# Differential-attention layer: the turn of the fourth attention tile placed behind the low parts of v, the turn of the gated rows one slot sooner, and the weighted values in two PSUM banks

## The chip, the cores and the metric

The kernel runs on one NeuronCore of a Trainium2 chip. The metric is the device time of one execution in microseconds (us). The execution that the profiler recorded has its own time; the rows below are from it.

## What is computed

The reference is one decoder layer over 512 rows of 2048 float32 values. It is cut here to what matters:

```
proj = x @ w_in                           # [512, 4*2048]: q | k | v | z
# 8 head pairs; in each two heads of q and k (128 wide) and one v, z (256 wide)
logits = q_h @ k_h.T / sqrt(128) + rel_bias[distance], causal
a = softmax(logits_0) - lam * softmax(logits_1)
o = a @ v                                 # [512, 256] for each pair
o = rms_norm(o, subln_g) * (1 - lam_init)
y = (o * silu(z)) @ w_out
out = layer_norm(2**0.25 * x + y, ln_g, ln_b)
```

## The kernel before, in words

**Split products.** Every float32 operand of a large product is held as a high part (ScalarE, ACT, copies it to the fp32r type) and a low part (VectorE, DVE, subtracts the high part from the original). TensorE (PE) makes three products per pair of operands: high by high, high by low and low by high.

**Pairs and slots.** The 2048 columns are worked in 8 head pairs `p`. For each pair PE goes through 16 slots `j`, each one slice of `w_in` of 512 KB and 24 matmuls of 512 columns. Slots 0 to 3 make q (PSUM tensor `proj`, banks 0 and 1), slots 4 to 7 make k (banks 2 and 3), slots 8 to 15 make v and z together (all four banks, one per tile `s` of 128 rows). In slot 15, the sum of tile s is final when its bank's last matmul ends (`vz_done`), and ACT then takes it out (`vz_tiles`, lines 441 to 450): exp of z, a copy of z, and the high part of v (`vz_hi`). DVE takes the low part of v (line 624, `vz_moved`). The next pair's slot 0 writes banks 0 and 1 again, so PE waits at line 908 until the low parts of tiles 0 and 1 have been taken; slot 4 waits for all four.

**What runs beside.** PE also makes the scores of pair p in slots 9 to 12 (`scores_of`), and the weighted values `a @ v` of pair p-1 in slots 0 to 3 of pair p (`weigh_v`, one row tile `t` per slot, 3, 6, 9 and 12 matmuls of 256 columns). All of them go to one PSUM bank, `av = att[:, 3]`; `weigh_v(t)` waits for `gated_ready` of tile t-1, since ACT (`norm`, the sum of squares) and DVE (`gate`, the product with silu(z) and the scale) read that bank.

**The order on VectorE.** The order of each engine is written out by hand. In slot j DVE makes the low part of the weight slice that PE needs three slots later (`split_lo_at`, line 601, `w_ready`), then in `late_steps` work of the pair before: in slot 0 silu of tiles 0 and 1, in slots 1 and 2 the low part of the turned attention tile j+1 (`aT_split`), in slots 1 to 4 `gate` of tile j-1 (which waits for two small operations on GpSimd, POOL), in slots 1 and 2 silu of tile j+1, and in slot 5 `turn_gated`. The attention matrix is turned by VectorE in blocks of 32 by 32, 16 instructions for each call of `turn` (line 672). `turn_a_early` (slot 13) turns the 6 blocks of row tiles 0 to 2. `turn_a_late` (slot 14, behind `combine(p, 3)`) turns the 4 blocks of row tile 3, which `aT_split(p, 3)` reads in slot 2 of the next pair. Slot 15 has `split_lo_at` and `aT_split` of tiles 0 and 1, and then `vz_tiles` follows. `q_chunk` (the low part of q) stands behind `late_steps` in slot 4.

**The loops.** Pair 0 is written out; on PE pairs 1 to 7 are one loop (line 994), on ACT and DVE pairs 1 to 6 are a loop and pair 7 is written out. SyncE (SP) loads one weight slice per slot into a ring of four; the load of a slice waits for `w_ready` of the slice four before it. Behind pair 7 comes the output projection: chunk c = 0 has 8 slots `i` with the same late steps of pair 7 between them. Slot i needs the split of g, the gated, normed and turned rows, for its two k tiles (`g_split`, line 811). The tiles of pair 7 itself are used in slot 7; they come from `turn_gated` (slot 5), `g_copy` on ACT (slot 6) and the split behind it. Chunks 1 to 3 have 192 matmuls each and go by turns to `att` and `proj`.

Of the kernel before, what the change touches and what calls it, by code (L numbers as in the profile page):

```python
# [34 lines left out]
ACT = mybir.ActivationFunctionType  # L35
# [7 lines left out]
PW = D // PAIRS  # L43
HD = PW // 2
ST = SEQ // P
# [30 lines left out]
def diff_layer(nc, x, rel_bias, lam_q1, lam_k1, lam_q2, lam_k2, subln_g, ln_g, ln_b, x_cols, w_in_tiles,  # L76
               w_out_tiles, out):
    with ExitStack() as ctx:  # L78
        def sb(name, shape, dt=F32):
            return ctx.enter_context(nc.sbuf_tensor(name, shape, dt))  # L80

        def sem(name):
            return ctx.enter_context(nc.semaphore(name))
# [25 lines left out]
        silu_z = scratch[:, 1024:2048].rearrange("p (t e) -> p t e", t=ST)  # L109
        a_rows = scratch[:, 2048:2048 + A_TILES * P].rearrange("p (n c) -> p n c", n=A_TILES)  # L110
        gated = scratch[:, 2048:3072].rearrange("p (t e) -> p t e", t=ST)
# [21 lines left out]
        inv_sum = sb("inv_sum", [P, ST, 2])  # L133
# [4 lines left out]
        o_scale = sb("o_scale", [P, ST])  # L138
# [9 lines left out]
        proj = ctx.enter_context(nc.psum_tensor("proj", [P, 4, 512], F32))  # L148
        att = ctx.enter_context(nc.psum_tensor("att", [P, 4, 512], F32))
        scores = att[:, 0:2]  # L150
        av = att[:, 3, 0:PW]

        g_banks, b_banks = proj, att

# [56 lines left out]
        gated_ready = sem("gated_ready")  # L211
# [205 lines left out]
        def _(act):  # L417
# [47 lines left out]

            def norm(p, t):
                act.wait_ge(av_done, p * ST + t + 1)
                nc.scalar.activation(gated[:, t], av, ACT.Square, scale=inv_sum[:, t, 0:1],  # L468
                                     accum_out=sq_sum[:, t:t + 1]).then_inc(sq_ready, 1)

            def g_copy(p):
# [124 lines left out]
        def _(dve):  # L596
            def split_lo_at(p, j):

                a = j + LEAD
                dve.wait_ge(w_hi, p * QUARTERS + a + 1)  # L600
                nc.vector.tensor_tensor(split_view(a, 1), w_raw[:, ring(a)],  # L601
                                        split_view(a, 0).bitcast(F32), ALU.subtract).then_inc(w_ready, 1)
# [12 lines left out]
            def k_chunk(p):  # L615
                for e in range(2):
                    dve.wait_ge(k_hi, 2 * p + e + 1)
                    nc.vector.tensor_tensor(kT[:, 1, e], proj[:, 2 + e], kT[:, 0, e].bitcast(F32),  # L618
                                            ALU.subtract).then_inc(k_moved, 1)

            def vz_tiles(p):
                for s in range(ST):
                    dve.wait_ge(vz_hi, p * ST + s + 1)
                    nc.vector.tensor_tensor(v[:, 1, s], proj[:, s, 0:PW], v[:, 0, s].bitcast(F32),  # L624
                                            ALU.subtract).then_inc(vz_moved, 1)

            def silu(p, t):

                part = silu_z[:, t]
                dve.wait_ge(vz_hi, p * ST + t + 1)  # L630
                nc.vector.tensor_scalar(part, part, 1.0, None, ALU.add).then_inc(z_denom, 1)
                dve.wait_ge(z_denom, p * ST + t + 1)
                nc.vector.reciprocal(part, part).then_inc(z_inv, 1)  # L633
                dve.wait_ge(z_inv, p * ST + t + 1)
                nc.vector.tensor_tensor(part, part, z_rows[:, t], ALU.mult).then_inc(silu_ready, 1)

            def logits_of(p, t):
                dve.wait_ge(scores_done, p * ST + t + 1)
                if not (isinstance(p, int) and p == 0 and t == 0):
                    dve.wait_ge(a_ready, p * ST + t)  # L640
                if t == 0:
                    dve.wait_ge(bias_loaded, p * 16 + 16)
                    if not (isinstance(p, int) and p == 0):
                        dve.wait_ge(g_ready, p)
                dve.sem_inc(tile_begun, 1)
                for h in range(2):
                    nc.vector.tensor_tensor_reduce(  # L647
                        out=logits[:, h, 0:(t + 1) * P], in0=scores[:, h, 0:(t + 1) * P],
                        in1=bias[:, h, (ST - 1 - t) * P:SEQ], scale=1.0, scalar=LOWEST,
                        op0=ALU.add, op1=ALU.max, accum_out=row_max[:, h:h + 1]).then_inc(max_ready, 1)  # L650
                dve.wait_ge(max_ready, (p * ST + t + 1) * 2)
                nc.vector.tensor_scalar(neg_max[:], row_max[:], -1.0, None, ALU.mult).then_inc(neg_max_ready, 1)  # L652
# [15 lines left out]
            def turn(dst, src):  # L668

                for i in range(P // B):  # L670
                    for j in range(P // B):
                        last = nc.vector.transpose(dst[j * B:(j + 1) * B, ..., i * B:(i + 1) * B],  # L672
                                                   src[i * B:(i + 1) * B, ..., j * B:(j + 1) * B])
                return last
# [8 lines left out]
            def turn_a_late(p):  # L683

                dve.wait_ge(a_ready, p * ST + ST)
                turn(aT_late, a_rows[:, A_EARLY:A_TILES]).then_inc(aT_done, 1)

            def turn_gated(p):

                dve.wait_ge(gated_ready, p * ST + ST)  # L690
                turn(gT, gated_tiles).then_inc(nT_done, 1)

            def aT_split(p, t):
                dve.wait_ge(aT_hi, p * ST + t + 1)
                cols = slice(0, (t + 1) * P)
                nc.vector.tensor_tensor(aT[:, t % 2, 1, cols], turned_a(t).rearrange("p n c -> p (n c)"),  # L696
                                        aT[:, t % 2, 0, cols].bitcast(F32), ALU.subtract).then_inc(aT_ready, 1)

            def gate(p, t):
                n = p * ST + t + 1  # L700
                dve.wait_ge(rms_ready, n)
                nc.vector.tensor_tensor(o_scale[:, t:t + 1], rms[:, t:t + 1], inv_sum[:, t, 0:1],
                                        ALU.mult).then_inc(o_scale_ready, 1)
                dve.wait_ge(o_scale_ready, n)
                dve.wait_ge(silu_ready, n)
                if t == 0:
                    dve.wait_ge(aT_done, 2 * p + 2)
                nc.vector.scalar_tensor_tensor(gated[:, t], av, o_scale[:, t:t + 1], silu_z[:, t],
                                               ALU.mult, ALU.mult).then_inc(gated_ready, 1)

            def late_steps(p, j):
                if j == 0:
                    silu(p, 0)
                    silu(p, 1)
                if j in (1, 2):
                    aT_split(p, j + 1)
                if 1 <= j <= 4:
                    gate(p, j - 1)
                if j in (1, 2):
                    silu(p, j + 1)  # L720
                if j == 5:
                    turn_gated(p)

            def slot(p, j, late):
                if j == VZ:
                    k_chunk(p)
                if 10 <= j < 13:
                    logits_of(p, j - 10)
                if j == 13:
                    combine(p, 2)  # L730
                    logits_of(p, 3)
                split_lo_at(p, j)
                if late:
                    late_steps(p - 1, j)
                if j in (10, 11):
                    combine(p, j - 10)
                if j == (7 if isinstance(p, int) and p == 0 else 4):
                    q_chunk(p)
                if j == 13:
                    turn_a_early(p)  # L740
                if j == 14:
                    combine(p, 3)
                    turn_a_late(p)
                if j == 15:
                    aT_split(p, 0)
                    aT_split(p, 1)
# [129 lines left out]
        def _(pe):  # L876
            def mm(dst, lhsT, rhs, start, stop):
                return nc.tensor.matmul(dst, lhsT, rhs, start=start, stop=stop, skip_group_check=True)  # L878
# [83 lines left out]
            def weigh_v(p, t):  # L962
                pe.wait_ge(aT_ready, p * ST + t + 1)
                pe.wait_ge(vz_moved, p * ST + t + 1)
                if not (isinstance(p, int) and p == 0 and t == 0):
                    pe.wait_ge(gated_ready, p * ST + t)
                dst = av
                for kt in range(t + 1):
                    cols = slice(kt * P, (kt + 1) * P)
                    a_hi, a_lo = aT[:, t % 2, 0, cols], aT[:, t % 2, 1, cols]  # L970
                    mm(dst, a_hi, v[:, 0, kt], kt == 0, False)
                    mm(dst, a_hi, v[:, 1, kt], False, False)
                    last = mm(dst, a_lo, v[:, 0, kt], False, kt == t)
                last.then_inc(av_done, 1)
# [130 lines left out]
```

## Time and profile before

| | |
|---|---|
| median of 3 runs | 991.6 us (989.1 to 991.71) |
| the profiled execution: its own time | 991.09 us |
| its span, first to last instruction | 989.2 us |
| mean granted TensorE clock | 0.981 of full speed |
| PE busy | 951.7 us (96%) |
| DVE busy | 601.8 us (61%) |
| ACT busy | 317.5 us (32%) |
| POOL busy | 66.1 us (7%) |

The span is what the rows add up to; 1.9 us of the execution's own time lie outside it. A busy PE is busy at whatever clock was granted to it, so the granted clock is read beside the busy share.

### The profile page before, as it was taken

To read this page: it belongs to the slowest core of one execution; us is meant where nothing else is said; L and a number is where in the kernel's file an instruction comes from. 1 tells how busy PE (TensorE), PEld (TensorE's weight loads), DVE (VectorE), ACT (ScalarE), POOL (GpSimd) and SP (SyncE) were. 2 spreads that over 40 slices of the span, in tenths; PEclk is the share of its full clock that TensorE was granted. 3 is DMA by queue.
4 is the path that set the end of the run, shared out by engine and by line. 5 is a ranking of instruction groups with operands and counts; after the bars stand their busy time and mean duration, and the time that the engine had idled before them with its cause. 6 is when DMAs were issued, how large, how long until landed. Compare 5 with 4: busy or idle time off the path is not lost.

```text
span 989.2 us, 11790 instructions
## 1 busy us (share of the span) xinstructions
PE 951.7 (96%) x4288; PEld 790.2 (80%) x4288; DVE 601.8 (61%) x1142; ACT 317.5 (32%) x556; POOL 66.1 (7%) x133
## 2 busy tenths in 40 slices
PE   8999999999999999899989998999899989999996
PEld 7888788878887888788878887888788868788884
DVE  4537753775377537853785378537853796434475
ACT  4424222422242224322432243224322433222311
POOL 2100100010001000110011001100100011000022
PEclk9999999999999999999999999999999989999998
DMA  8731243124312332233123222422232221633423
GB/s 303 254 103 65 85 136 105 64 85 134 104 64 85 133 103 67 85 133 103 66 85 133 97 73 85 133 96 74 85 106 99 71 85 64 234 128 106 149 93 120
DMA packets 33367, 108.62 MB, mean 110 GB/s; under 512 B 4272, under 2 KB 5296, under 8 KB 33088
## 3 DMA queue, kind: packets, MB, share of 16 engines
q1 hardware_dynamic: 28896, 94.65, 28.3%
q0 software_dynamic: 2336, 9.48, 2.8%
q10 hardware_dynamic: 2112, 4.19, 1.2%
q8 instruction: 13, 0.21, 0.1%
q14 instruction: 10, 0.08, 0.0%
HBM read 104.07 MB, written 9.48 MB: 115 GB/s over the span
## 4 chain that ended last, share of the span: by engine, by line
PE 80%; DVE 15%; issue 2%; DMA 1%; SPq 0%; ACT 0%; POOLq 0%; POOL 0%; DVEq 0%; ACTq 0%
PE proj L878 66%; PE att L878 15%; DVE scratch L672 9%; DVE w_split L601 2%; DMA w_raw<-w_in_tiles_dram 1%; DVE scratch L647 1%; DVE scratch L664 1%; DVE operands L696 0%; DVE operands L624 0%; SPq L297 0%; DVE operands L751 0%; SPq L292 0%; DVE mix L660 0%; POOLq L78 0%; POOL big L411 0%
## 5 line engine op out<-in xcount | busy, mean ns | idle before, releaser
L878 PE MATMUL proj<-w_split,xg_split 128*128 128x512 f32 x1872 | 433.1, 390 | 2.5 <-DVE xg_split L811 2.5
L878 PEld LDWEIGHTS proj<-w_split,xg_split 128*128 128x128 f32 x1872 | 350.0, 188 | 74.7 <-issue 2.9
L878 PE MATMUL proj<-xg_split,w_split 128*128 128x512 f32 x1536 | 367.5, 399 | 19.1 <-DVE operands L624 18.0
L878 PEld LDWEIGHTS proj<-xg_split,w_split 128*128 128x128 f32 x1536 | 293.8, 193 | 84.0 <-DVE operands L624 20.9
L424 ACT ACTIVATE w_split<-w_raw 128x1024 fp32r<-128x1024 f32 x128 | 135.8, 1061 | 389.2 <-PE proj L878 382.2
L601 DVE TENSOR_TENSOR w_split<-w_raw,w_split 128x1024 fp32r<-128x1024 f32 x128 | 156.8, 1225 | 122.8 <-ACT w_split L424 120.9
L672 DVE STREAM_TRANSPOSE scratch<-scratch 32x192 f32<-32x192 f32 (+2 forms) x384 | 141.8, 369 | 5.2
L647 DVE CUSTOM_DVE_ANT_0 scratch<-att,bias 128x128 f32<-128x128 f32 (+3 forms) x64 | 28.9, 489 | 113.3 <-PE att L878 113.3
L878 PE MATMUL att<-operands 128*128 128x256 f32 (+3 forms) x432 | 69.0, 299 | 0.0
L878 PEld LDWEIGHTS att<-operands 128*128 128x128 f32 x432 | 64.0, 190 | 6.2
L831 DVE TENSOR_TENSOR w_split<-w_raw,w_split 128x1024 fp32r<-128x1024 f32 x25 | 30.6, 1225 | 61.3 <-ACT w_split L567 61.3
L878 PE MATMUL att<-w_split,xg_split 128*128 128x512 f32 x288 | 66.1, 389 | 0.0
L878 PEld LDWEIGHTS att<-w_split,xg_split 128*128 128x128 f32 x288 | 54.1, 188 | 11.2
L399 POOL TENSOR_SCALAR mean_sq<-sq_sum 128x1 f32<-128x1 f32 x32 | 12.6, 392 | 739.5 <-ACT scratch L468 739.5
L567 ACT ACTIVATE w_split<-w_raw 128x1024 fp32r<-128x1024 f32 x25 | 26.5, 1060 | 96.9 <-PE proj L878 61.0
L633 DVE RECIPROCAL scratch<-scratch 128x256 f32<-128x256 f32 x32 | 56.1, 1753 | 1.1
L456 ACT ACTIVATE scratch<-scratch,neg_max 128x128 f32<-128x128 f32 (+3 forms) x64 | 35.5, 556 | 38.9 <-DVE neg_max L652 38.9
L618 DVE TENSOR_TENSOR operands<-proj,operands 128x512 fp32r<-128x512 f32 x16 | 10.3, 686 | 28.8 <-ACT operands L439 28.8
L402 POOL TENSOR_TENSOR rms<-mean_sq,minus_half 128x1 f32<-128x1 f32 x32 | 22.7, 710 | 2.7
L878 PE MATMUL att<-operands,xg_split 128*128 128x512 f32 x96 | 22.4, 389 | 0.0
L878 PEld LDWEIGHTS att<-operands,xg_split 128*128 128x128 f32 x96 | 18.0, 188 | 3.7
L463 ACT ACTIVATE operands<-scratch 128x128 fp32r<-128x128 f32 (+3 forms) x32 | 13.9, 459 | 19.2 <-DVE scratch L672 19.2
(73 smaller groups left out, 393.6 us busy)
## 6 DMA issues: line engine op xcount, KB each, us to landing
w_raw<-w_in_tiles_dram SPq DMA_DIRECT2D x126, 512.0 KB, 3.3
w_raw<-w_out_tiles_dram SPq DMA_DIRECT2D x32, 512.0 KB, 3.3
bias_by_distance<-bias_lines POOLq DMA_DIRECT2D x8, 640.0 KB, 6.4
bias<-bias_by_distance POOLq DMA_DIRECT2D x8, 512.0 KB, 5.2
x_res<-in_x_dram ACTq DMA_DIRECT2D x4, 1024.0 KB, 5.6
out_dram<-big SPq DMA_DIRECT2D x16, 256.0 KB, 2.7
big<-x_cols_dram SPq DMA_DIRECT2D x7, 512.0 KB, 8.9
scratch<-in_ln_g_dram SPq DMA_DIRECT2D x1, 1024.0 KB, 5.8
```

What stands on the lines that cost most here:

```text
L399: nc.gpsimd.tensor_scalar(mean_sq[:, t:t + 1], sq_sum[:, t:t + 1], 1.0 / PW, EPS, ALU.mult, ALU.add).then_inc(mean_ready, 1)
L402: nc.gpsimd.tensor_tensor(rms[:, t:t + 1], mean_sq[:, t:t + 1], minus_half[:], ALU.pow).then_inc(rms_ready, 1)
L424: nc.scalar.activation(split_view(a, 0), w_raw[:, ring(a)], ACT.Copy).then_inc(w_hi, 1)
L456: nc.scalar.activation(e, e, ACT.Exp, bias=neg_max[:, h:h + 1], accum_out=row_sum[:, h:h + 1]).then_inc(exp_ready, 1)
L463: nc.scalar.activation(aT[:, t % 2, 0, 0:(t + 1) * P], turned_a(t).rearrange("p n c -> p (n c)"), ACT.Copy).then_inc(aT_hi, 1)
L567: nc.scalar.activation(out_split_view(n, 0), w_raw[:, ring(n)], ACT.Copy).then_inc(w_hi, 1)
L601: nc.vector.tensor_tensor(split_view(a, 1), w_raw[:, ring(a)], split_view(a, 0).bitcast(F32), ALU.subtract).then_inc(w_ready, 1)
L633: nc.vector.reciprocal(part, part).then_inc(z_inv, 1)
L647: nc.vector.tensor_tensor_reduce(out=logits[:, h, 0:(t + 1) * P], in0=scores[:, h, 0:(t + 1) * P], in1=bias[:, h, (ST - 1 - t) * P:SEQ], s ...
L672: last = nc.vector.transpose(dst[j * B:(j + 1) * B, ..., i * B:(i + 1) * B], src[i * B:(i + 1) * B, ..., j * B:(j + 1) * B])
L831: nc.vector.tensor_tensor(out_split_view(n, 1), w_raw[:, ring(n)], out_split_view(n, 0).bitcast(F32), ALU.subtract).then_inc(w_ready, 1)
L878: return nc.tensor.matmul(dst, lhsT, rhs, start=start, stop=stop, skip_group_check=True)
```

## The change

Four edits. DVE's `turn_a_late(p)` moves from slot 14 to the end of `vz_tiles(p)`, behind the low parts of v. `turn_gated(p)` moves from slot 5 to slot 4, which puts it ahead of `q_chunk` there. `av` becomes two banks, `att[:, 2:4]`, tile t in bank t % 2, in `weigh_v`, `norm` and `gate`. `weigh_v(t)` waits no more for tile t-1 to be gated but, from t = 2 on, for tile t-2.

```diff
-        av = att[:, 3, 0:PW]
+        av = att[:, 2:4, 0:PW]
...
             def norm(p, t):
-                nc.scalar.activation(gated[:, t], av, ACT.Square, scale=inv_sum[:, t, 0:1],
+                nc.scalar.activation(gated[:, t], av[:, t % 2], ACT.Square, scale=inv_sum[:, t, 0:1],
...
             def vz_tiles(p):
                 for s in range(ST):
                     dve.wait_ge(vz_hi, p * ST + s + 1)
                     nc.vector.tensor_tensor(v[:, 1, s], proj[:, s, 0:PW], v[:, 0, s].bitcast(F32),
                                             ALU.subtract).then_inc(vz_moved, 1)
+                turn_a_late(p)
...
-                nc.vector.scalar_tensor_tensor(gated[:, t], av, o_scale[:, t:t + 1], silu_z[:, t],
+                nc.vector.scalar_tensor_tensor(gated[:, t], av[:, t % 2], o_scale[:, t:t + 1], silu_z[:, t],
...
-                if j == 5:
+                if j == 4:
                     turn_gated(p)
...
                 if j == 14:
                     combine(p, 3)
-                    turn_a_late(p)
...
             def weigh_v(p, t):
                 pe.wait_ge(aT_ready, p * ST + t + 1)
                 pe.wait_ge(vz_moved, p * ST + t + 1)
-                if not (isinstance(p, int) and p == 0 and t == 0):
-                    pe.wait_ge(gated_ready, p * ST + t)
-                dst = av
+                if t >= 2:
+                    pe.wait_ge(gated_ready, p * ST + t - 1)
+                dst = av[:, t % 2]
```

## Rows read from the trace of the kernel before

**Rows 1.** The page: busy times of the engines, and the first queue of instruction fetches.
```profile
PE 951.7 (96%) x4288; PEld 790.2 (80%) x4288; DVE 601.8 (61%) x1142; ACT 317.5 (32%) x556; POOL 66.1 (7%) x133
...
q8 instruction: 13, 0.21, 0.1%
```

**Rows 2.** The waits, whole span: waiter, whom for: us in total, times, longest.
```profile
DVE o_scale L702 <- POOL rms L402: 18.3, 32, 0.7
...
PE proj L878 <- DVE operands L624: 22.5, 8, 4.6
```

**Rows 3.** Timeline, from pair 5 to pair 6: start, length, engine, what [idle before].
```profile
577.34 16.48 PE L878 MATMUL proj<-w_split,xg_split 128*128 128x512 f32 x72
...
588.42 1.06 ACT L424 ACTIVATE w_split<-w_raw 128x1024 fp32r<-128x1024 f32 x1 [1.34 <-PE proj L878]
588.84 5.05 DVE L672 STREAM_TRANSPOSE scratch<-scratch 32x128 f32<-32x128 f32 x16
...
591.69 0.39 ACT L450 ACTIVATE operands<-proj 128x256 fp32r<-128x256 f32 x1
...
593.92 1.23 DVE L601 TENSOR_TENSOR w_split<-w_raw,w_split 128x1024 fp32r<-128x1024 f32 x1
...
594.41 0.39 ACT L450 ACTIVATE operands<-proj 128x256 fp32r<-128x256 f32 x1
594.67 1.07 ACT L424 ACTIVATE w_split<-w_raw 128x1024 fp32r<-128x1024 f32 x1
...
595.60 1.41 DVE L624 TENSOR_TENSOR operands<-proj,operands 128x256 fp32r<-128x256 f32 x4
...
596.40 7.25 PE L878 MATMUL proj<-xg_split,w_split 128*128 128x512 f32 x24 [2.58 <-DVE operands L624]
596.92 1.22 DVE L601 TENSOR_TENSOR w_split<-w_raw,w_split 128x1024 fp32r<-128x1024 f32 x1
...
604.79 1.23 DVE L601 TENSOR_TENSOR w_split<-w_raw,w_split 128x1024 fp32r<-128x1024 f32 x1 [1.74 <-ACT w_split L424]
```

**Rows 4.** Windows: stretch, its length, busy by engine, granted clock, DMA share, GB/s.
```profile
593.80:596.40 2.60, 0.03 (x1) 0.00 (x0) 2.57 (x7) 1.88 (x4) 0.00 (x0) 0.96 0.06 14
596.40:603.70 7.30, 7.29 (x26) 5.91 (x27) 6.51 (x9) 0.00 (x1) 0.00 (x0) 0.78 0.40 139
...
840.60:843.10 2.50, 0.03 (x1) 0.01 (x1) 1.35 (x2) 2.47 (x4) 0.00 (x0) 1.00 0.59 197
...
849.00:979.00 130.00, 130.00 (x576) 107.61 (x574) 64.20 (x75) 27.98 (x31) 10.38 (x9) 1.00 0.38 134
```

**Rows 5.** Timeline of slots 1 to 5 of pair 6.
```profile
607.23 0.48 DVE L708 SCALAR_TENSOR_TENSOR scratch<-att,o_scale,scratch 128x256 f32<-128x256 f32 x1
...
609.32 0.88 PE L878 MATMUL att<-operands 128*128 128x256 f32 x6
...
610.03 5.63 PE L878 MATMUL proj<-xg_split,w_split 128*128 128x512 f32 x24
...
615.50 1.24 PE L878 MATMUL att<-operands 128*128 128x256 f32 x9
...
631.37 7.17 DVE L672 STREAM_TRANSPOSE scratch<-scratch 32x256 f32<-32x256 f32 x16
```

**Rows 6.** Timeline from the end of pair 7 through chunk 0 of the output.
```profile
775.40 16.48 PE L878 MATMUL proj<-w_split,xg_split 128*128 128x512 f32 x72
...
796.45 7.87 PE L878 MATMUL proj<-w_split,operands 128*128 128x512 f32 x24 [4.57 <-DVE operands L624]
797.21 1.22 DVE L811 TENSOR_TENSOR xg_split<-big,xg_split 128x1024 fp32r<-128x1024 f32 x1
...
820.54 1.22 DVE L811 TENSOR_TENSOR xg_split<-big,xg_split 128x1024 fp32r<-128x1024 f32 x1
...
832.08 7.17 DVE L672 STREAM_TRANSPOSE scratch<-scratch 32x256 f32<-32x256 f32 x16
...
843.12 5.69 PE L878 MATMUL proj<-w_split,xg_split 128*128 128x512 f32 x24 [2.49 <-DVE xg_split L811]
```

## The prediction

> **What bounds the kernel now.** I began with the page: PE is busy for 951.7 of 989.2 us, DVE for 601.8 [rows 1]. So PE is the bound on average, and only two things can shorten the span: time in which PE stands still, and time in which it runs at the lower clock. The waits say where it stands still: 22.5 us in 8 waits for line 624, the low part of v [rows 2], and 2.49 us in one wait for line 811, the split of g [rows 6]. Eight is the number of pair ends, so I opened the timeline of one of them [rows 3]. PE's last matmul of pair 5 ends at 577.34 + 16.48 = 593.82; slot 0 of pair 6 starts at 596.40, after 2.58 us. It waits for the low parts of v tiles 0 and 1, which DVE starts only at 595.60. ACT had tile 1's high part ready at 591.69 + 0.39 = 592.08. DVE was not waiting: from 588.84 to 593.89 it made the 16 turns of the fourth attention tile, then the weight split and two attention splits (593.92 to 595.60), and only then the low parts. The wait is thus the length of DVE's queue, and the turns are the part of it that nobody needs yet: their reader, `aT_split(3)`, comes in slot 2 of the next pair.
>
> The windows show a second cost. Slot 0 behind the wait runs at a mean granted clock of 0.78, between the chip's levels of 1.2 and 2.4 GHz, and the stretch without PE work stands right before it [rows 4]. Its 24 matmuls take 7.25 us against 5.63 for those of slot 2 [rows 3, 5]: 1.62 us lost. So a pair end costs 2.58 + 1.62 = 4.20 us. At the end of pair 7 it is dearer: 4.57 us of waiting and 7.87 - 5.63 = 2.24 us of slow matmuls [rows 6], 6.81 us.
>
> **Part 1, the turn moved behind the low parts (the main term).** Nothing is removed: the same 16 instructions, 5.05 us, run later. In front of them, slot 15's weight split now waits for ACT's high part, done at 588.42 + 1.06 = 589.48. The split and the two attention splits take 595.60 - 593.92 = 1.68 us, to about 591.2. Low parts take 1.41 us for four, so 0.4 each: tile 0 at 591.6, tile 1 from 592.1 (ACT's high part) to 592.5, tile 3 from 594.80 (ACT, 594.41 + 0.39) to 595.2. PE needs tiles 0 and 1 at 593.82: ready 1.3 us before. The wait of 2.58 us goes, and with no stretch without work before slot 0 I take the low clock to go too. What says that the clock can stay up: PE ran 130 us without a pause at 1.00, and a pause of 2.49 us in chunk 0 left it at 1.00 [rows 4]. The 2.58 us at the pair end are only slightly longer, so any remaining wait well below them should be harmless.
>
> What is behind the moved turns in DVE's queue? They now run from 595.3 to 600.3, and slot 0 of the next pair (weight split, two silus) comes after them. In the trace it runs from 596.92 to 604.79 - 1.74 = 603.05, that is 6.1 us [rows 3]. Shifted: 600.3 to 606.4. Slot 1 from its split (604.79) to the end of `gate(0)` (607.23 + 0.48) is 2.9 us, in which a wait for POOL of about 0.45 us lies (18.3 us in 32 over the span [rows 2]) that falls away when PE is early. So `gate(0)` ends at 608.8. PE, starting at 593.82 with 5.47 us for a slot (610.03 to 615.50 in the trace [rows 5]) and 0.71 for the 6 matmuls that weight tile 1 (609.32 to 610.03; so 0.36 for each 3, 0.36, 1.07 and 1.43 for the other tiles), is at the weighting of tile 2 at 611.3. The slack is 2.5 us. `gate(1)` follows a silu ((6.13 - 1.22) / 2 = 2.45 us) and the next slot's 2.5 us behind, at 613.8, and the weighting of tile 3 comes at 617.8: slack 3.9 us. Slot 0's weight split ends at 601.5, and PE needs it in slot 3 after 612. SP's load behind that split starts about 6 us later against PE than now, for a slice that ACT reads four slots on, over 20 us; the view of waits has no wait of PE for a load. The splits of slots 14 and 15, and their loads, only come earlier. So per pair end the whole 4.20 us are gained at seven pair ends.
>
> I check the sum against the view of waits: 22.5 - 4.57 = 17.9 us for seven, and 7 x 1.62 = 11.3 us of clock. Together **29.2 us**.
>
> **Part 2, two banks for the weighted values.** No instruction is added; one wait per tile becomes weaker. Before, the weighting of tile 1 waited for `gate(0)`, which ended at 607.71, and started at 609.32: no wait shown, slack 1.6 us [rows 5]. By itself this edit is worth nothing. After part 1 it is needed: PE comes to the weighting of tile 1 at 605.1, and `gate(0)` ends at 608.8. With one bank, PE would wait 3.7 us there at every pair. With two it waits for tile t-2 alone. So I count it 0, as the cover that part 1 uses up.
>
> **Part 3, the gated rows turned in slot 4.** Their 16 turns take 7.17 us [rows 5] and now precede the low part of q (1.2 us) and the weight split of slot 5. Inside the pairs: the weighting of tile 3 ends near 619.3. Even if `gate(3)` came a whole slot later, at 624.8, the turns would end at 632.0, q at 633.2, the split at 634.4. PE needs q's banks and this slice in slot 8, at 619.3 + 4 x 5.47 = 641.2. The slack is at least 6.8 us: 0. ACT's `g_copy` and POOL's bias load are not delayed. The edit matters in chunk 0 only.
>
> **Part 4, the end of pair 7 and chunk 0.** PE ends pair 7 at 775.40 + 16.48 = 791.88 [rows 6]. Everything up to the turns lies as in pair 5, 198.06 us later, but two splits for g (`g_early_lo`, 1.2 us each) stand where the turns stood, from 786.9 to 789.3. The weight split and two attention splits end at 791.0, the low parts of tiles 0 and 1 at 791.4 and 791.8 (a near tie, but only tile 0 holds the first matmul back, since chunk 0 waits tile by tile), tile 3's at 793.3. So slot i = 0 starts at 791.9 at full clock, a gain of 6.81 us. DVE turns the fourth tile from 793.3 to 798.35 and starts its slot 0 at 798.35 against 797.21, 1.14 us later, in a stretch in which it is busy up to 820.54 [rows 6] but for the waits for POOL, 0.45 us at each of three gates. PE being earlier, these vanish. So DVE comes to the split of tile pair 6 at 820.54 + 1.14 less 1.35, near 820.4, then 1.2 for it, 1.2 for the weight, 0.7 for `gate(3)`, and turns the gated rows from 823.6 to 830.75. From the end of these turns to PE's start on slot 7 it is 843.12 - 839.25 = 3.87 us now, so PE can start slot 7 at 834.6. Its own path is 791.88 + 7 x 5.47 + 0.35 + 0.71 + 1.07 + 1.43 = 833.7. A wait of **0.9 us** stays, where 2.49 us stood. `gate(0)` and the weighting of tile 2 are nearly tied here (809.1, by the count of part 1 with a split of g more, against 791.88 + 3 x 5.47 + 1.07 = 809.4). Slot 7 starts at 834.6 instead of 843.12: **8.5 us** for this part, the 6.81 among them. Behind it, 3 x 192 matmuls and the tail are as before.
>
> **Sum.** 29.2 + 8.5 = 37.7 us. The span comes to 951.5 us, the execution's time to 991.09 - 37.7 = 953.4. The profiled execution is 0.5 us below the median; I say 953.5.
>
> **Bounds.** Nothing below 22.5 + 2.5 + 11.3 + 2.3 = 38.6 us less is in reach, since PE works without pause at 1.00 elsewhere: 952.5, and with the scatter of the runs shown 950.5. The upward side of the unknown: the slack of 1.3 us at the pair end could be used up by a start that I do not see (the trace shows no pair end without a wait), and the near ties in chunk 0. One us at each of 8 pair ends gives 961.5.
>
> **Rivals.**
>
> *The loop's jump comes to light.* Six of the eight pair ends are a jump back on PE (iterations 1 to 7 of its loop). It may hide below the 2.58 us of waiting today; then up to those 2.58 us remain as a pause, with the low clock behind it, and six pair ends gain nothing: 953.5 + 6 x 4.2 = 979. Against it: ACT jumps back between 594.41 and 594.67, at the pitch of its other copies, and DVE has slot 0's split at 596.92 right behind the last low part, 595.60 + 1.41 [rows 3]. The fetch queue moved 13 packets in the whole span [rows 1], which does not look like seven passes of a long body. The Trainium skill, in "Runtime: NRT & Kernel Launch", section "Instruction fetch mechanics", says that a taken branch to a target outside the fetched pages must wait for a fetch from memory; by that rule this rival would hold. The rows of ACT and DVE do not show such a wait, and no row shows PE's. Chance 0.07.
>
> *The pause goes, the slow slot stays*, because the clock falls for something else at this place, such as the DMA share of 0.40 in that window. For: it falls at every pair end. Against: chunk 0's pause window has a DMA share of 0.59 at 1.00 [rows 4]. It gives back 7 x 1.62 + 2.24 = 13.6 us: 967. Chance 0.05.
>
> *Slower: DVE's queue holds PE at the weighting of tile 2.* The moved turns push the weight split, the silus and `gate(0)` behind the pair end. If `gate(0)` ended more than 2.5 us later than I have it, PE would wait there; past 2.5 + 4.2 = 6.7 us the pair is longer than before. If the turns took twice their 5.05 us and ran beside slower silus, 8.5 us late say, a pair would cost 1.8 us more, and 8 pairs 14: 1006. Against it: every length in the chain is measured in this place. Chance 0.03.
>
> *No change*: PE's restart hangs on something besides line 624 that ends at the same moment. Its weight slice was split in slot 13 and ACT is done with tile 1 at 592.08, so I see none. 991.6, chance 0.03.
>
> **How the numbers follow.** The forecast has 0.82 with its own range of 950.5 to 962; the three rivals that leave that range and the no-change case have 0.18 together, so this range stands. A measurement of this kernel can tell about 0.3%, 3 us, from no change. Faster by more: forecast, jump and clock, 0.94. Same 0.03, slower 0.03.
>
> **What the profile after would show.** Right: no PE wait for line 624, or a few tenths; slot 0 of each pair in about 5.5 us at clock 1.00; PE's starts of slot 0 4.2 us closer together; DVE's 16 turns of 32x128 right behind the low parts; the weight split of slot 15 right behind ACT's high part and not 4.4 us behind it; mean clock above 0.995; one PE wait for line 811 of about 0.9 us near 834. Wrong: a pause of over 1 us at the pair end with a new releaser or "issue" (jump), slot 0 still near 7.2 us without a pause (clock), a PE wait on `att` for line 708 or 696 (DVE's queue).

## The result and the profile after

The changed kernel takes 950.86 us (median of 4 runs, 950.42 to 950.97) against 990.35 us for the kernel before on the same chip (4 runs, 988.68 to 991.71). The ratio is 0.9601, 95% interval 0.9582 to 0.9620: 4.0% faster. The forecast was 953.5 us in a range of 950.5 to 962.0.

The page of the changed kernel, its head and its row of the granted clock:

```profile
span 949.0 us, 11790 instructions
## 1 busy us (share of the span) xinstructions
PE 936.8 (99%) x4288; PEld 782.0 (82%) x4288; DVE 600.1 (63%) x1142; ACT 316.6 (33%) x556; POOL 61.8 (7%) x133
...
PEclk9999999999999999999999999999999999999998
```

The instructions are as many as before. DVE does the same 600 us of work as in [rows 1]. PE is busy for 14.9 us *less* than before although it does the same matmuls: that is the part of the gain that no count of waits shows, since a matmul at the low clock counts as busy for longer (the 24 of slot 0 took 7.25 us at a mean clock of 0.78 [rows 3, 4] and take 5.60 now). The rest, 989.2 - 949.0 - 14.9 = 25.3 us, is PE time that was idle.

The waits of PE in the changed kernel (waiter, whom for: us in total, times, longest), to be held against [rows 2]:

```profile
PE att L986 <- POOL minus_half L368: 1.5, 1, 1.5
PE proj L878 <- DVE xg_split L811: 0.5, 1, 0.5
PE proj L878 <- DVE w_split L769: 0.2, 1, 0.2
```

The eight waits for line 624 are gone, and no wait on `att` for the gate has come in their place. What is left after the opening is one wait of half a microsecond in chunk 0.

The same pair end as in [rows 3], now some 25 us earlier (PE's slot 0 at 571.14 for 596.40). Columns of the timeline: start, length, engine, what, and in brackets the idle time before:

```profile
565.90 1.06 ACT L424 ACTIVATE w_split<-w_raw 128x1024 fp32r<-128x1024 f32 x1 [1.34 <-PE proj L878]
567.00 1.23 DVE L601 TENSOR_TENSOR w_split<-w_raw,w_split 128x1024 fp32r<-128x1024 f32 x1 [0.71 <-ACT w_split L424]
...
568.14 0.62 DVE L697 TENSOR_TENSOR operands<-scratch,operands 128x128 fp32r<-128x128 f32 x2
...
568.68 0.42 DVE L624 TENSOR_TENSOR operands<-proj,operands 128x256 fp32r<-128x256 f32 x1
...
569.59 0.42 DVE L624 TENSOR_TENSOR operands<-proj,operands 128x256 fp32r<-128x256 f32 x1 [0.50 <-ACT operands L450]
...
570.95 0.42 DVE L624 TENSOR_TENSOR operands<-proj,operands 128x256 fp32r<-128x256 f32 x1 [0.94 <-ACT operands L450]
571.14 5.60 PE L878 MATMUL proj<-xg_split,w_split 128*128 128x512 f32 x24
...
572.31 0.42 DVE L624 TENSOR_TENSOR operands<-proj,operands 128x256 fp32r<-128x256 f32 x1 [0.94 <-ACT operands L450]
572.65 5.04 DVE L673 STREAM_TRANSPOSE scratch<-scratch 32x128 f32<-32x128 f32 x16
576.58 0.52 PE L878 MATMUL att<-operands 128*128 128x256 f32 x3
...
582.40 0.88 PE L878 MATMUL att<-operands 128*128 128x256 f32 x6
...
585.66 0.48 DVE L709 SCALAR_TENSOR_TENSOR scratch<-att,o_scale,scratch 128x256 f32<-128x256 f32 x1
...
588.58 1.24 PE L878 MATMUL att<-operands 128*128 128x256 f32 x9
...
590.43 0.48 DVE L709 SCALAR_TENSOR_TENSOR scratch<-att,o_scale,scratch 128x256 f32<-128x256 f32 x1
...
595.12 1.59 PE L878 MATMUL att<-operands 128*128 128x256 f32 x12
```

Read it in three steps. DVE now waits for ACT at the low parts of tiles 1 to 3, so it is DVE that is early. The low part of tile 1 is there at 570.01, 1.1 us before PE's first matmul of slot 0 at 571.14, which has no bracket: PE has not paused. The 16 turns follow from 572.65, and the queue behind them reaches the gate of tile 0 at 585.66 + 0.48 = 586.14. PE starts to weight tile 1 at 582.40, *before* that gate, which one bank would forbid; and tile 2 at 588.58, 2.4 us behind it.

The windows of both kernels over one pair, from start of slot 0 to start of slot 0 (stretch, length, busy time of PE, PEld, DVE, ACT and POOL, granted clock, DMA share, GB/s), first the kernel before:

```profile
497.40:596.40 99.00, 96.42 (x438) 80.24 (x438) 62.10 (x128) 32.21 (x61) 5.69 (x10) 0.98 0.28 97
```

and the changed kernel:

```profile
476.40:571.10 94.70, 94.70 (x440) 79.29 (x439) 61.99 (x128) 32.10 (x61) 4.82 (x10) 1.00 0.30 101
```

The windows are rounded to a tenth of a microsecond. By the rows of PE the starts of slot 0 of pairs 1 to 7 lay 99.02 to 99.15 us apart before, 99.08 in the mean, and all lie 94.65 apart now: a pair is 4.4 us shorter at the same work, without idle time and at full clock. The rest of the gain is in chunk 0 of the output projection, the changed kernel:

```profile
785.92 1.22 DVE L811 TENSOR_TENSOR xg_split<-big,xg_split 128x1024 fp32r<-128x1024 f32 x1
...
791.75 7.19 DVE L673 STREAM_TRANSPOSE scratch<-scratch 32x256 f32<-32x256 f32 x16
...
802.82 5.72 PE L878 MATMUL proj<-w_split,xg_split 128*128 128x512 f32 x24 [0.45 <-DVE xg_split L811]
```

DVE turns the gated rows from 791.75 to 798.94, and PE starts on slot 7 at 802.82, which is 3.88 us later, as it was before (3.87). One more place in chunk 0 is close: `gate(0)` ends at 777.64 and PE begins to weight tile 2 at 777.88, so 0.24 us of slack is left there, where the prediction counted 0.3.

### The profile page after: what moved, and what is told of

Read it like the earlier page. It is cut to its first block, busy times and chain, and to the rows that moved or that the text cites. A ratio compares the mean times of both kernels' runs of the same rounds, so it can differ in the third digit from the quotient of the medians.

```text
span 949.0 us, 11790 instructions
## 1 busy us (share of the span) xinstructions
PE 936.8 (99%) x4288; PEld 782.0 (82%) x4288; DVE 600.1 (63%) x1142; ACT 316.6 (33%) x556; POOL 61.8 (7%) x133
## 3 DMA queue, kind: packets, MB, share of 16 engines
q1 hardware_dynamic: 28896, 94.65, 29.3%
## 4 chain that ended last, share of the span: by engine, by line
PE 93%; DVE 4%; DMA 1%; ACT 0%; issue 0%; SPq 0%; POOLq 0%; POOL 0%; ACTq 0%
PE proj L878 78%; PE att L878 15%; DVE scratch L673 1%; DVE xg_split L811 1%; DVE scratch L634 1%; DVE w_split L831 1%; DMA big<-x_cols_dram 1%; DVE scratch L709 0%; SPq L297 0%; POOLq L78 0%; POOL big L411 0%; DVE xg_split L607 0%; ACT xg_split L553 0%; DVE operands L697 0%; ACT xg_split L428 0%
## 5 line engine op out<-in xcount | busy, mean ns | idle before, releaser
L878 PE MATMUL proj<-xg_split,w_split 128*128 128x512 f32 x1536 | 356.1, 390 | 0.3 <-DVE w_split L769 0.2
L878 PEld LDWEIGHTS proj<-xg_split,w_split 128*128 128x128 f32 x1536 | 287.1, 188 | 59.5 <-issue 0.6
L399 POOL TENSOR_SCALAR mean_sq<-sq_sum 128x1 f32<-128x1 f32 x32 | 8.4, 262 | 708.4 <-ACT scratch L468 708.4
L624 DVE TENSOR_TENSOR operands<-proj,operands 128x256 fp32r<-128x256 f32 x32 | 13.4, 421 | 17.6 <-ACT operands L450 17.5
L402 POOL TENSOR_TENSOR rms<-mean_sq,minus_half 128x1 f32<-128x1 f32 x32 | 22.5, 704 | 2.7
```

The lines of the kernel that those rows point to most:

```text
L402: nc.gpsimd.tensor_tensor(rms[:, t:t + 1], mean_sq[:, t:t + 1], minus_half[:], ALU.pow).then_inc(rms_ready, 1)
```

## The experiments

Eight kernels in two groups of four; each group was timed in turns with the kernel before on one chip. The first three undo or do one part alone, the fourth asks for the price of the clock, and the last four set the pause or the slack to a chosen length.

**one_bank.** The changed kernel without its second PSUM bank.

```diff
-        av = att[:, 2:4, 0:PW]
+        av = att[:, 3, 0:PW]
...
-                if t >= 2:
-                    pe.wait_ge(gated_ready, p * ST + t - 1)
-                dst = av[:, t % 2]
+                if not (isinstance(p, int) and p == 0 and t == 0):
+                    pe.wait_ge(gated_ready, p * ST + t)
+                dst = av
```

> The changed kernel with the weighted values back in one PSUM bank and the old wait of each tile for the one before. Theory (the second bank is what lets the moved turns pay): PE comes to the weighting of tile 1 some 11.3 us behind its start on slot 0 (582.40 against 571.14 in the changed kernel) and gate(0) ends 15.0 us behind it (586.14), so a pause of 3.7 us opens there in each of 8 pairs: 8 x 3.9 = 31 us over 950.9, that is 982. If the clock falls behind this pause as it did behind the 2.6 us at the pair end, 8 x 1.6 or more comes on top: 995, as slow as the kernel before or slower. Rival (the bank edit does nothing): 951.

Measured: 1000.57 us, ratio 1.0106 (1.0091 to 1.0120), slower than the kernel before. Its waits of PE, and the timeline of PE at three of the eight places, the last of them in chunk 0:

```profile
PE att L878 <- DVE scratch L709: 31.8, 8, 5.9
```

```profile
113.41 1.14 PE L878 MATMUL att<-operands 128*128 128x256 f32 x6 [3.72 <-DVE scratch L709]
114.35 7.05 PE L878 MATMUL proj<-xg_split,w_split 128*128 128x512 f32 x24
...
213.60 1.62 PE L878 MATMUL att<-operands 128*128 128x256 f32 x6 [3.73 <-DVE scratch L709]
...
215.01 7.89 PE L878 MATMUL proj<-xg_split,w_split 128*128 128x512 f32 x24
...
820.35 1.62 PE L878 MATMUL att<-operands 128*128 128x256 f32 x6 [5.89 <-DVE scratch L709]
821.77 6.65 PE L878 MATMUL proj<-w_split,xg_split 128*128 128x512 f32 x24
```

The pause is the one that was worked out, 3.7 us, at seven of eight places (5.9 us at the last). The span is 49.6 us over that of the changed kernel; 31.8 of it is pause, and most of the rest, some 17 us, is the low clock. Against 0.88 and 5.63 us at full clock, the two groups behind a pause are together 1.7 to 1.8 us longer at five of the eight places and 2.8 to 3.0 us at the other three. The estimate of 1.6 us a pause was too small because of those three. The length of the pause does not explain them: the longest pause, 5.9 us, is among the five, and in the pairs 1.7 and some 2.9 take turns behind pauses of the same 3.7 us. What decides between the two these runs do not show. The moved turns without the second bank are a loss: the two edits are one.

**gated_slot5.** The changed kernel with `turn_gated` in slot 5 (`if j == 5:` for `if j == 4:`).

> The changed kernel with the gated rows turned in slot 5 as before. Theory: inside the pairs it changes nothing; in chunk 0 the turns wait for slot 5's weight split, which waits for ACT's high part (done at 792.64), so they end about 2.1 us later, and PE's wait for line 811 grows from 0.45 to about 2.5 us: 953.0. Rival (the edit does nothing, or helps inside the pairs): no difference from 950.9, or a difference of several us spread over the pairs.

Measured: 953.93 us (952.62 to 954.64), ratio 0.9633 (0.9621 to 0.9646), 3.1 us over the changed kernel. The wait of PE for line 811 is back at 2.5 us; the turns start at 794.28 instead of 791.75. The timeline of this kernel:

```profile
794.28 7.18 DVE L673 STREAM_TRANSPOSE scratch<-scratch 32x256 f32<-32x256 f32 x16
...
805.32 5.70 PE L878 MATMUL proj<-w_split,xg_split 128*128 128x512 f32 x24 [2.50 <-DVE xg_split L811]
```

Inside the pairs no wait appeared. So this edit is worth the 2.05 us between the two waits, in chunk 0 alone; half a microsecond of the span's difference of 2.5 us lies in the opening: PE starts its first long stretch at 12.74 for 12.23, a start that the ten traces place between 12.07 and 12.82. The pause of 2.50 us left the clock up in this trace (5.70 us behind it). Three of the five runs took 953.93 to 954.64 us at a mean clock of 0.994 or 0.995, against 0.998 in the traced one; a fall of the clock behind the same pause would do that, but no trace of them shows it.

**no_move.** The kernel before with the two banks and the gated rows in slot 4; the turns of the fourth tile stay in slot 14.

> The kernel before with two banks and the gated rows in slot 4, but the turns of the fourth tile left in slot 14. Theory (the move is the main term, the other two edits have only chunk 0 to give): all 8 waits for line 624 stay at 22.5 us, slot 0 stays slow, the wait for line 811 of 2.49 us goes: 2.5 us under before, 0.9975. Rival (the second bank pays by itself): under 0.99.

Measured: 988.10 us, ratio 0.9977 (0.9968 to 0.9986). Its waits of PE:

```profile
PE proj L878 <- DVE operands L624: 22.5, 8, 4.6
```

The 22.5 us stand as in [rows 2], and the wait for line 811 is not in the list. The two lesser edits without the move are worth 2 us; the move (with its bank) is worth the rest.

**fill10.** The kernel before with ten matmuls of no use ahead of the wait. It leaves nothing out and adds sums that nobody reads.

```diff
+                if j == 0 and not opening:
+                    for _ in range(10):
+                        mm(att[:, 2], xg_split[:, 0, 0, 0:P], xg_split[:, 0, 1], True, True)
                 if part == 0 and not opening:
                     pe.wait_ge(vz_moved, p * ST - 2 + 2 * c)
```

> The kernel before with 10 matmuls of 512 columns into a free PSUM bank put on PE in front of the wait of slot 0, in the seven pair ends of the loop; their sums are read by nobody. They fill 2.2 us of the pause of 2.58 us and take none of the waiting away. Theory (the slow slot 0 is the price of the pause alone): the granted clock stays at 1.00 in slot 0, which then takes 5.5 us, and the time falls by 7 x 1.62 = 11.3 us: 979, 0.9886. Rival (the clock falls for another cause at this place, as the load of DMA): no change, 990.

Measured: 980.81 us, ratio 0.9906 (0.9891 to 0.9922). The timeline of PE at one pair end and at slot 7 of chunk 0; then the windows of slot 0 at that pair end, and of the first slot and of slot 7 of chunk 0, where nothing was filled in:

```profile
198.33 5.74 PE L878 MATMUL proj<-xg_split,w_split 128*128 128x512 f32 x24 [0.30 <-DVE operands L624]
...
831.30 7.29 PE L878 MATMUL proj<-w_split,xg_split 128*128 128x512 f32 x24 [2.49 <-DVE xg_split L811]
```

```profile
198.30:203.80 5.50, 5.47 (x24) 4.54 (x25) 5.40 (x8) 0.00 (x0) 0.00 (x0) 1.00 0.57 191
...
785.40:792.50 7.10, 7.09 (x26) 5.80 (x27) 7.00 (x10) 0.00 (x0) 0.00 (x0) 0.79 0.41 146
...
831.30:838.60 7.30, 7.30 (x25) 5.89 (x26) 3.26 (x3) 1.44 (x2) 0.00 (x0) 0.77 0.62 225
```

PE waits for the same low part as before. Only the 2.2 us of work in the pause differ, and slot 0 runs at 1.00, with a DMA share of 0.57, while the unfilled end of pair 7 still has its 4.57 us pause and a clock of 0.79 behind it. So the slow slot is the price of the pause and not of something else at this place. The starts of slot 0 lie 97.51 us apart for 99.08 before, which is 11.0 us over seven pairs, near the 11.3 us expected. That the whole kernel gained only 9.4 us (10.2 us by the spans) has its cause in chunk 0: the pause of 2.49 us ahead of slot 7, which left the clock up in the kernel before (5.69 us behind it), brought it down here at nearly the same DMA share (0.58 for 0.59 in the pause), and the slot takes 7.29 us. Slot 0 of chunk 0 is 0.8 us shorter (7.08 for 7.87), and 11.0 + 0.8 - 1.6 are the 10.2 us of the spans. Useless work made this kernel 0.9% faster.

**ahead8, ahead12, ahead14.** The pause as a dial: of the 16 turns, 8, 12 or 14 go back ahead of the low parts in pairs 0 to 6. The edit of ahead12 in the changed kernel is this one; `turn` gets a third argument there, the part of its 16 instructions to issue, and the other two kernels have 8 or 14 for 12:

```diff
                 if j == 14:
                     combine(p, 3)
+                    if not (isinstance(p, int) and p == PAIRS - 1):
+                        dve.wait_ge(a_ready, p * ST + ST)
+                        turn(aT_late, a_rows[:, A_EARLY:A_TILES], slice(0, 12))
...
-                turn(aT_late, a_rows[:, A_EARLY:A_TILES]).then_inc(aT_done, 1)
+                rest = slice(0, 16) if isinstance(p, int) and p == PAIRS - 1 else slice(12, 16)
+                turn(aT_late, a_rows[:, A_EARLY:A_TILES], rest).then_inc(aT_done, 1)
```

> The changed kernel with 8 of the 16 turns of the fourth tile back in slot 14, 8 behind the low parts, in pairs 0 to 6 (pair 7 as in the changed kernel). With 16 ahead the pause was 2.58 us; each turn is 0.316 us, so with 8 it should be 0.05 us, or none. Theory: 951, up to 1.5 us more.

Measured: 953.26 us, ratio 0.9626 (0.9610 to 0.9642), 2.4 us over the changed kernel and a little more than expected. The timeline at a pair end:

```profile
193.50 5.32 PEld L882 LDWEIGHTS proj<-xg_split,w_split 128*128 128x128 f32 x24 [0.44 <-DVE operands L624]
193.50 5.74 PE L882 MATMUL proj<-xg_split,w_split 128*128 128x512 f32 x24
```

PE shows no idle time at all, and still the pair takes 94.96 us (98.54 to 193.50), 0.31 us more than in the changed kernel. The weight loads show the wait that the matmuls hide.

> As the last, but with 12 of the 16 turns ahead in pairs 0 to 6. The pause should be 2.58 - 4 x 0.316 = 1.3 us, seven times. Theory A (a pause of this length leaves the clock up): 7 x 1.5 = 10 us over the changed kernel, 961, slot 0 at clock 1.00. Theory B (any pause here brings the low clock): 7 x 1.6 more, 972.

Measured: 962.00 us, ratio 0.9714 (0.9698 to 0.9730). The seven pauses are 1.24 to 1.28 us and slot 0 takes 5.73 to 5.78 us in each: theory A.

```profile
196.02 5.73 PE L882 MATMUL proj<-xg_split,w_split 128*128 128x512 f32 x24 [1.28 <-DVE operands L624]
```

> As the last, but with 14 of the 16 turns ahead. The pause should be 1.95 us, seven times. Theory A (the clock stays up up to some length between this and 2.58 us): 7 x 2.1 = 15 us over the changed kernel, 966. Theory B (the clock falls here too): 977. All 16 ahead would be 981 with pair 7 as in the changed kernel.

Measured: 974.36 us (973.21 to 976.21), ratio 0.9846 (0.9830 to 0.9862), between the two theories. The windows of slot 0 at the seven pair ends say why:

```profile
100.50:106.00 5.50, 5.50 (x24) 4.53 (x25) 5.32 (x10) 0.04 (x1) 0.00 (x0) 1.00 0.54 183
197.40:202.90 5.50, 5.50 (x17) 4.36 (x18) 5.32 (x10) 0.00 (x0) 0.00 (x0) 0.69 0.50 184
295.90:301.40 5.50, 5.50 (x24) 4.58 (x25) 5.32 (x10) 0.00 (x0) 0.00 (x0) 1.00 0.50 184
392.70:398.20 5.50, 5.47 (x17) 4.37 (x18) 5.32 (x10) 0.03 (x1) 0.00 (x0) 0.69 0.52 185
491.20:496.70 5.50, 5.49 (x17) 4.40 (x18) 5.32 (x10) 0.01 (x1) 0.00 (x0) 0.69 0.54 185
589.70:595.20 5.50, 5.50 (x17) 4.37 (x18) 5.32 (x10) 0.00 (x0) 0.00 (x0) 0.69 0.51 184
688.20:693.70 5.50, 5.50 (x24) 4.56 (x25) 5.32 (x10) 0.00 (x0) 0.00 (x0) 1.00 0.49 183
```

Seven pauses of 1.88 to 1.92 us, the same work before and behind each: at four of them the clock fell, at three it did not. Neither theory holds as a rule for each pause of this length; what the difference between the seven is, these runs do not show. The four runs, 973.21 to 976.21 us at mean clocks of 0.990 to 0.986, lie 3 us apart, where those of ahead12 lie within 0.5 us, so the number of falls seems to differ from run to run; only the fastest of them was traced.

**twice.** The changed kernel with 16 more turns of the same blocks on DVE, into a part of `x_res` that nobody reads, in front of the moved ones. It is extra work; nothing is left out.

```diff
+                turn(x_res[:, 2].rearrange("p (n c) -> p n c", n=ST), a_rows[:, A_EARLY:A_TILES])
                 turn(aT_late, a_rows[:, A_EARLY:A_TILES]).then_inc(aT_done, 1)
```

> The changed kernel with 16 more turns of the same blocks in front of the moved ones, into a free part of x_res that nobody reads: 5.05 us more on DVE behind each pair end, in the place from which the forecast's slower rival would act. gate(0) ends 2.4 us before the weighting of tile 2 in the changed kernel, so a pause of about 2.6 us should open there. Theory (the slack is as counted, 2.4 us): 8 x 2.8 = 22 us more, 973, and 8 x 1.6 on top if the clock falls, 986. Rival (the slack is larger, the queue catches up elsewhere): under 960.

Measured: 986.97 us (984.76 to 989.15), ratio 0.9967 (0.9955 to 0.9978). Its waits of PE, and the timeline at one pair and in chunk 0:

```profile
PE att L879 <- DVE scratch L710: 21.8, 8, 3.7
```

```profile
217.05 2.26 PE L879 MATMUL att<-operands 128*128 128x256 f32 x9 [2.60 <-DVE scratch L710]
...
812.90 1.32 PE L879 MATMUL att<-operands 128*128 128x256 f32 x9 [3.68 <-DVE scratch L710]
```

The pause at tile 2 is the 2.6 us that were worked out at seven of eight places, 2.50 to 2.61; in chunk 0, where the slack was smaller to begin with, it is 3.7. So the slack of the changed kernel inside the pairs is the 2.4 us that its timeline shows. With the clock the 16 turns too many cost 36 us and nearly the whole gain. The slower rival's mechanism exists and sits where it was put; the changed kernel stays on the right side of it by 2.4 us. It is also nearer than the prediction had it: that put the point at which a pair is as long as before at 6.7 us of lateness and counted no clock behind the pause. Here DVE is 5.05 us late and a pair takes 98.77 to 99.00 us, nearly the 99.08 of the kernel before.

## Why the prediction was right

**The wait and its cause.** The pause at the pair end was DVE's queue, and the queue ends 1.1 us ahead of PE now (forecast 1.3). This is shown by experiments and not by the trace alone: no_move has the other edits and keeps the pause and nearly all of the time, and ahead12 and ahead14 bring the pause back by as much as the turns put ahead (1.28 us for 1.3 worked out, 1.91 for 1.95).

**The clock as a second cost.** Forecast as 1.62 us a pair on top of 2.58. Fill10 shows it by itself, and PE's busy time fell by 14.9 us against the 11.3 + 2.2 us put down to it; the other 1.4 us are met by the 0.16 us for each of eight pauses that are explained under the term that was off. The rival "the slow slot stays" falls with both. One sentence beside it does not hold: that a wait well below 2.58 us should be harmless. The changed kernel has no pause there and so did not need it; ahead12 bears it out at 1.28 us, and ahead14 answers it at 1.9 us, where the clock fell at four of seven places.

**The queue behind the pair end.** `gate(0)` was put at 15.0 us behind PE's start and came 586.14 - 571.14 = 15.0 behind; its slack was put at 2.5 us and is 2.4. The slack at tile 3 was put at 3.9 us and is 595.12 - 590.91 = 4.2.

**The second bank counted at nothing, as cover.** With one bank a wait of 3.7 us was worked out; one_bank has 3.72. What was missing in that sentence of the prediction is the clock: it spoke of the pause alone, and the loss was 6.2 us a pair in the mean (49.6 / 8, with the longer pause in chunk 0).

**The gated rows.** Counted 0 inside the pairs and right. In chunk 0 the wait was forecast at 0.9 us and is 0.45: DVE came to these turns 31.3 us behind PE's start on chunk 0 (760.44), by the count 31.7, and most of these 0.4 us is lengths in its chain that were rounded up.

**The jump.** The rival that the loop's jump would come to light is answered by the changed kernel's PE at the last jump, from pair 6 to pair 7:

```profile
663.75 2.20 PE L878 MATMUL proj<-w_split,xg_split 128*128 128x512 f32 x9
665.79 5.60 PE L878 MATMUL proj<-xg_split,w_split 128*128 128x512 f32 x24
```

The next slot starts at 665.79, the slot before ends at 665.95: the jump costs nothing that can be seen. The other five jumps show as little, since all starts of slot 0 from pair 1 to chunk 0 are 94.65 us apart, those with a jump between them and the last one without. The fetch that the Trainium skill describes in "Runtime: NRT & Kernel Launch", section "Instruction fetch mechanics", does not stand in PE's way here.

**The term that was off.** The sum was 37.7 us, the spans differ by 40.2. Seven pair ends gave 30.9 us where 29.2 were forecast (in the chain of waits PE's start on slot 4 of pair 1 moved from 128.26 in the kernel before to 123.49, that of pair 7 from 722.65 to 691.37, which is 31.28 us; 0.35 us of it is a faster opening). The two rows of PE at the jump, above, name most of the difference of 0.24 us a pair: in unbroken work the rows of two neighbouring groups overlap by 0.16 us, since a matmul's row runs on while the next has begun. A pause measured from the end of one row to the start of the next is therefore 0.16 us too short, eight times. The rest is the slow slot, put at 7.25 - 5.63 = 1.62 us by one pair end: over the seven it took 7.29 us in the mean, and in unbroken work it takes 5.60, which makes 1.69. Ahead8 shows the same from the other side, 0.31 us a pair with no idle time in PE's rows. Chunk 0 with the end of pair 7 gave 9.0 us for 8.5, which is for the most part the shorter wait for line 811.

**The floor that was broken.** The prediction held nothing below 952.5 us to be in reach, since pauses and low clock by the rows came to 38.6 us, and stretched the range to 950.5 by the scatter of the runs. The spans differ by 40.2 us, and all four runs lie below 952.5. The floor was too high for the reasons just given: the rows showed each pause 0.16 us short and one slow slot stood for all. The median, 950.86, is in the range by 0.36 us, and by an allowance that was made for another reason; that much is luck. One step of the arithmetic is off as well: from 953.4 us for the profiled execution to a median 0.5 us above it is 953.9, not 953.5.

## What to carry to other kernels

When the bound engine waits for a short operation on another one, look at what stands ahead of it in that engine's queue, and for each piece when its result is read: a piece whose reader comes late belongs behind. Then count the queue again on the far side, for the moved piece uses up slack there, and the buffer that frees it (here one PSUM bank) is part of the move and not an extra: without it this change loses 1%. Where TensorE pauses, add to the pause what its clock costs behind it, and read busy time at two clocks with care; if a pause cannot be removed, work of no use in it may already pay.

## What the runs showed that was not expected

- Whether the clock falls goes with the length of the pause: behind none of seven pauses of 1.3 us, behind four of seven of 1.9 us, behind 21 of 24 of 2.5 to 2.6 us, behind all twelve from 3.6 us up (all traces together).
- What a fall costs does not simply grow with it: some 1.6 us behind those of 1.9 us, 1.4 to 1.8 behind those of 2.5 to 2.6, 1.7 or 2.8 to 3.0 behind those of 3.7, 2.2 behind the pause of 4.57 us in the kernel before and 1.4 behind the same pause in fill10, 1.8 behind that of 5.9.
- Near 2.5 us neither answer is fixed. In no_move a pause of 2.53 us left slot 0 at full speed (5.74 us), and the next, of 2.57 us, did not (7.31 us). In the kernel before, the pause at the first of these places was 2.54 us, and slot 0 took 7.33. The rows of PE in no_move:

```profile
100.66 5.74 PE L878 MATMUL proj<-xg_split,w_split 128*128 128x512 f32 x24 [2.53 <-DVE operands L624]
198.17 7.31 PE L878 MATMUL proj<-xg_split,w_split 128*128 128x512 f32 x24 [2.57 <-DVE operands L624]
```

- The pause with no clock behind it that the prediction took from chunk 0 (2.49 us at 1.00) was thus weaker evidence than it seemed: the same length can go either way, and in fill10 the pause at that very place, 2.49 us again, did bring the clock down.
